# All large tiles moved to multiples of 2 KB, and the head norms computed with the tokens in the partitions

## What is computed

```python
def rms_norm(x, g):
    y = xf * lax.rsqrt(jnp.mean(xf * xf, axis=-1, keepdims=True) + EPS)
    return (y * g).astype(x.dtype)

# first layer: h = rms_norm(x, norm_mix); h @ w_in is split into heads
aq = rms_norm(aq.reshape(b, t, 4, 2, 64), a_q_norm)      # ak alike; heads of 64
out_a = rms_norm(diff_attention(aq, ak, av, ...), a_subln)   # 4 heads of 128
bq = rms_norm(bq.reshape(b, t, 3, 4, 128), b_q_norm)     # bk alike; windowed attention
ck = rms_norm(kv[:, :, 0], c_k_norm)                     # 256 memory tokens
cq = rms_norm(cq.reshape(b, t, 4, 128), c_q_norm)
x = x + sum(gates * branches) @ w_out
x = x + (silu(h2 @ w_ffn_gate) * (h2 @ w_ffn_up)) @ w_ffn_down
# second and third layer, each:
x = x + 0.5 * swiglu(rmsnorm(x, ...), w1, w3, w2)
o = hgrn2_chunkwise(q, k, v, log_f)                      # 4 heads of 128
o = o * lax.rsqrt(jnp.mean(o * o, axis=-1, keepdims=True) + EPS) * norm_g * silu(g_in)
x = x + concat(o, multiscale_pool(u)) @ w_out
x = x + mem_cross_attention(rmsnorm(x, ...), rmsnorm(mem, ...), wq, wkv, wo)
x = x + 0.5 * swiglu(rmsnorm(x, ...), w1, w3, w2)
return rmsnorm(x, final_norm)
```

## Time and profile before

| | before |
|---|---|
| median of 3 runs | 3494.8 us (3493.5 to 3494.88) |
| the profiled execution | 3494.81 us, span 3493.0 us |
| TensorE busy, matmuls | 3339.0 us (96%) |
| TensorE busy, weight loads | 2691.4 us (77%) |
| VectorE busy | 1876.8 us (54%) |
| ScalarE busy | 1110.6 us (32%) |
| mean granted clock of TensorE | 0.982 |
| memory traffic | 313.41 MB, mean 90 GB/s |

### The profile page before, as it was taken

How to read it: one execution, slowest core, us unless ns; L and a number is a source line. 1 busy time by engine, 2 the same in 40 slices (tenths; PEclk the granted TensorE clock), 3 DMA queues, 4 the chain that set the end, 5 groups by cost and what they waited for, 6 DMA issues and landing times. The chain is left out here.

```text
span 3493.0 us, 39914 instructions
## 1 busy us (share of the span) xinstructions
PE 3339.0 (96%) x15102; PEld 2691.4 (77%) x15102; DVE 1876.8 (54%) x2458; ACT 1110.6 (32%) x1487; POOL 0.2 (0%) x4
## 2 busy tenths in 40 slices
PE   7889999999999999999899999999999989999998
PEld 6657777768888888888786888888888868778886
DVE  6666666555554455335764555345543576555543
ACT  3543444433222322232333322222222233332221
POOL 0000000000000000000000000000000000000000
PEclk9989999999999999999899999999999989999999
DMA  3222222322222222222231222222222223222222
GB/s 130 88 68 85 89 83 73 103 87 94 96 96 97 94 97 97 91 100 74 74 101 55 91 96 96 96 91 96 96 96 98 80 67 103 67 79 96 96 94 81
DMA packets 88824, 313.41 MB, mean 90 GB/s; under 512 B 9984, under 2 KB 10496, under 8 KB 88448
## 3 DMA queue, kind: packets, MB, share of 16 engines
q1 hardware_dynamic: 82080, 294.69, 25.3%
q10 hardware_dynamic: 6624, 17.03, 1.6%
HBM read 309.58 MB, written 2.10 MB: 89 GB/s over the span
## 5 line engine op out<-in xcount | busy, mean ns | idle before, releaser
L784 PE MATMUL ps<-x_hi,whi 128*128 128x512 f32 x2816 | 1121.8, 398 | 13.1 <-DVE wlo L1193 13.1
L786 PE MATMUL ps<-x_hi,wlo 128*128 128x512 f32 x2816 | 1101.0, 391 | 0.0
L785 PE MATMUL ps<-x_lo,whi 128*128 128x512 f32 x2816 | 1100.8, 391 | 0.0
L1011 ACT ACTIVATE whi<-raw 128x1024 fp32r<-128x1024 f32 x554 | 582.7, 1054 | 988.3 <-DMA raw<-in_weights 985.6
L1193 DVE TENSOR_TENSOR wlo<-raw,whi 128x1024 fp32r<-128x1024 f32 x554 | 676.1, 1222 | 374.5 <-ACT whi L1011 366.3
L784 PEld LDWEIGHTS ps<-x_hi,whi 128*128 128x128 f32 x2816 | 532.6, 189 | 132.7 <-DVE wlo L1193 13.2
L785 PEld LDWEIGHTS ps<-x_lo,whi 128*128 128x128 f32 x2816 | 532.5, 189 | 113.3 <-issue 5.7
L786 PEld LDWEIGHTS ps<-x_hi,wlo 128*128 128x128 f32 x2816 | 531.5, 189 | 113.3
L786 PE MATMUL ps<-h_hi,wlo 128*128 128x512 f32 x880 | 346.7, 394 | 0.0
L784 PE MATMUL ps<-h_hi,whi 128*128 128x512 f32 x880 | 346.7, 394 | 0.0
L785 PE MATMUL ps<-h_lo,whi 128*128 128x512 f32 x880 | 346.7, 394 | 0.0
(11 more groups left out here) (249 smaller groups left out, 3065.1 us busy)
## 6 DMA issues: line engine op xcount, KB each, us to landing
raw<-in_weights SPq DMA_DIRECT2D x554, 512.0 KB, 3.3
bias<-in_biasB ACTq DMA_DIRECT2D x16, 384.0 KB, 3.3
bias<-in_biasA ACTq DMA_DIRECT2D x16, 256.0 KB, 3.6
x_res<-in_x SPq DMA_DIRECT2D x8, 256.0 KB, 6.2
x_res<-in_x ACTq DMA_DIRECT2D x1, 2048.0 KB, 9.3
out_x<-x_res SPq DMA_DIRECT2D x8, 256.0 KB, 2.1
mem_raw<-in_mem ACTq DMA_DIRECT2D x1, 1024.0 KB, 4.6
mem_raw2a<-in_mem ACTq DMA_DIRECT2D x2, 512.0 KB, 3.9
```

The lines of the kernel that those rows point to most:

```text
L784: pe.matmul(out, hi, xhi, start=start, stop=False)
L785: pe.matmul(out, hi, xlo, start=False, stop=False)
L786: return pe.matmul(out, lo, xhi, start=False, stop=stop)
L1011: return act.activation(out, in_, ACT.Copy, scale=scale)
```

## The change

**Addresses.** The constants and small tiles are laid first, then the address is rounded up to a multiple of 2 KB, and the ring, x, x_hi, x_lo, `rstd_x`, `sq_sum` and `sq` follow. In the program as built `raw` is at 20480, x_hi at 69632, x_lo at 86016, `sq` at 106496 and the arena at 110592, all multiples of 2048; the arena's tiles keep their offsets in it. `rstd_mem` moves into the arena. The `rec` and `h_rec` tiles are gone.

**Head norms.** The square is now the stationary operand and a column of ones the moving one, for each block of 128 tokens: four small products (`hsum`) give the 128 x 4 sums with the tokens in the partitions (128 x 8 for A, two halves each). They go into a few columns of a PSUM bank of the jobs, the one after the next to be written. VectorE turns them into mean plus EPS and takes their reciprocal (`hinv`, 4 or 8 columns), ScalarE takes the root while it spreads each column over 128 (or 64) elements into `sd`, TensorE transposes the four blocks of `sd` into `O` (`hturn`), and VectorE multiplies the head by gain and `O` (`hscale`). Where there were two deferred steps in one flush there are now two flushes: sums one job after the square, transposes and scaling another job later. `settle` puts the inverses at the start of the next job; `drain` flushes until nothing is deferred.

**Order.** In `b_jobs` the value column of group 1 goes behind the keys of group 2, the last value column of the first head goes before the last split of A, and in the second pair of the mixer two key jobs of the memory move ahead of the scalings.

```diff
@@ class Schedule
+    def settle(self):
+        inverses, self.inverses = self.inverses, []
+        for id, form in inverses:
+            self.step("hinv", id=id, form=form, last=inverses[-1][0])
+        self.groups += 1
+
+    def hsums(self, id, ones, n, dim, sq):
+        form = dict(nt=n // P, w=2 if ones == "halves" else 1, dim=dim, slot=self.nsums % 4, k=self.nsums, group=self.groups)
+        self.nsums += 1
+        self.step("hsum", id=id, ones=ones, sq=sq, form=form, bank=(self.njobs + 1) % 3, behind=self.njobs - 2)
+        self.inverses.append((id, form))
+        return form
+
+    def hscale(self, id, form, /, **a):
+        self.settle()
+        self.step("hturn", id=id, form=form)
+        self.step("hscale", id=id, **a)
...
-        def rest():
-            step("hnorm", id=id, ones=ones, n=n, dim=dim, sq=sq)
-            step("hscale", id=id, src=src, gain=gain, n=n)
-        s.defer(rest)
+        def sums():
+            form = s.hsums(id, ones, n, dim, sq)
+            s.defer(lambda: s.hscale(id, form, src=src, gain=gain, n=n))
+        s.defer(sums)
...
-        return out
+        return [out[k] for k in (0, 1, 2, 3, 4, 6, 7, 5, 8)]
...
-    s.flush()
+    s.drain()
...
+        top[0] = (top[0] + 2 * KB - 1) // (2 * KB) * (2 * KB)
         raw_at = top[0]
...
@@ tensor
-                elif kind == "hnorm":
-                    pe.wait_ge(*on("hsq", a["id"]))
-                    wait_free("O")
-                    pe.matmul(O[:, 0:a["n"]], lhs[:, :], SQ[:, a["sq"], 0:a["n"]], start=True, stop=True)\
-                        .then_inc(*sig("hsum", a["id"]))
-                    free["O"] = ("hsd", a["id"])
+                elif kind == "hsum":
+                    pe.wait_ge(*on("hsq", a["id"]))
+                    if a["behind"] >= 0:
+                        pe.wait_ge(*on("evac", a["behind"]))
+                    picks = halves[:, 0:P:P // 2] if a["ones"] == "halves" else ones[:, 0:1]
+                    for c in range(form["nt"]):
+                        mm = pe.matmul(out[:, c * w:(c + 1) * w], SQ[:, a["sq"], c * P:(c + 1) * P], picks,
+                                       start=True, stop=True)
+                elif kind == "hturn":
+                    pe.wait_ge(*on("hsd", a["id"]))
+                    wait_free("O")
+                    for c in range(a["form"]["nt"]):
+                        mm = pe.transpose(O[:, c * P:(c + 1) * P], sd[:, c * P:(c + 1) * P], ident[:, :])
+                    free["O"] = ("hn", a["id"])
@@ scalar
-                    act.activation(sd[:, 0:a["n"]], O[:, 0:a["n"]], ACT.Sqrt, bias=EPS, scale=1.0 / a["dim"])
+                    act.activation(sd.rearrange("p (a b) -> p a b", a=cells),
+                                   inverse_of(form).rearrange("p (a b) -> p a b", b=1)
+                                   .broadcast_to([P, cells, P // form["w"]]), ACT.Sqrt).then_inc(*sig("hsd", a["id"]))
@@ vector
-                    dve.reciprocal(rec[:, 0:n], sd[:, 0:n]).then_inc(*sig("hrec", a["id"]))
+                    dve.wait_ge(*on("hsum", a["last"]))
+                    dve.tensor_scalar(inv, sums_at(sum_bank[a["id"]], form), 1.0 / form["dim"], EPS, ALU.mult, ALU.add)
+                    dve.reciprocal(inv, inv).then_inc(*sig("hinv", a["id"]))
...
-                    dve.scalar_tensor_tensor(buf(a["src"]), buf(a["src"]), gain_of(a["gain"]), rec[:, 0:n],
+                    dve.wait_ge(*on("hrt", a["id"]))
+                    dve.scalar_tensor_tensor(buf(a["src"]), buf(a["src"]), gain_of(a["gain"]), O[:, 0:n],
                                              ALU.mult, ALU.mult).then_inc(*sig("hn", a["id"]))
```

95 lines of the change are left out of this document (64 added, 31 removed).

## The result

The changed kernel takes 3455.47 us (median of 4 runs, 3454.62 to 3458.89), the kernel before, beside it, 3494.15 us (4 runs). The ratio is 0.989, with a 95% interval from 0.9877 to 0.9902: 39 us faster, where 164 were forecast. The profiled execution has a span of 3453.4 us. Lines have moved: the three products of a weight tile are now at 827, 828 and 829 (784, 785 and 786 before), the sums of the head norms at 889, their transposes at 898, ScalarE's root at 1148, VectorE's small pair at 1371 and 1374, the final multiply at 1379.

A forecast was written before the change was run, and what follows sets the result against it. TensorE, busy 96% of the span, was taken as the bound. From 3494.8 us, 162 for aligned addresses (172 less 10 given back) and 2 for head norms gave 3331 us, range 3297 to 3505.

The forecast's parts named there:

- The aligned product, 215 ns: Weight products with 512 columns: starts 215 ns apart once tiles are 2 KB-aligned, from 226.7 (x) and 233.3 (arena).
- its 95 us: Products reading x_hi or x_lo: 8110 at full clock, each 11.7 ns shorter, saving 95 us.
- the arena's 69 us: Products reading arena tiles (h, mix, xo, y, branch outputs): 3888 x 0.97, each 18.3 ns shorter, saving 69 us.
- Rival 1: 13 ns stay with every fp32r product, only the arena's 6.7 ns vanish: 26 us, 3467 us; chance 0.20 (3365 to 3475).
- The choice between two forms at offset 0: Aligned fp32r products: either no address loss, taken as 215 ns, or a loss of 64 columns, 240 ns.
- Products with 256 columns, 8 us: The shorter weight products: 768 save 9 ns each, 7 us, and the other 192 about 1 us.
- 10 us given back: Attentions and mixers, where TensorE waits for other engines: faster products only wait longer, cutting the address gain to 162 us.
- The head norms, -2 us: All 52 head norms: 22 us of transposes plus 4 of new waits less 28 of shorter waits; ends -20 and +25.
- the 9 us in each mixer: Recurrent mixers: some 9 of 21.9 us TensorE idle time in each vanish without the long reciprocal.
- the 10 us in the attentions: The two attentions: a quarter of TensorE's 41.3 us idle time saved, taken as 10 us.
- The new waits: Transposes waiting for sum, inverse and root where no job lies between: 3 us some four times, less earlier waits, 4 us.
- rival 2: Addresses do nothing: 3493 us, with the norms' ends 3475 to 3518; chance 0.10 together with rival 4, costlier norms.

The follow-up runs named there:

- The probe: Straight-line programs on TensorE alone, groups of 24 products with tile and weight addresses varied; fp32r with 512 columns took 226.7 ns at equal places, mostly 232.5 to 234.5 otherwise.
- the addresses alone: The kernel before with only the new 2 KB-aligned addresses and its old head norms: 3474.35 us, ratio 0.9942.
- the first program: Straight-line TensorE program in place of the model, 36 groups of 24 products varying offsets, columns, weight widths and types; fp32r with 512 columns took 226.7 ns at offset 0.
- the copies: New addresses with old head norms, each of the 52 VectorE reciprocals replaced by a plain copy of the same 512 elements: 3409.55 us, ratio 0.9756.
- a version 30 us faster: New addresses, old-form head norms without transposes, ScalarE making the inverse root by ln and exp from one table: 3425.07 us, ratio 0.9798.

## Why the prediction failed, by its steps

**The aligned product, 215 ns: wrong, and this is the miss.** It measures 226.7. The step took the 13.3 ns at x's offset for a part of the same address cost as h's 20 ns, and let both vanish at 0. The probe shows two costs: a fixed 13 ns of every fp32r product at the upper clock, and 6.7 ns where the moving tile and the weights stand differently in their 256 bytes. x paid only the first, so its 95 us were nothing; of the arena's 69 us there were 26 by the products and 20.4 by the clock on the wall. Rival 1 had this sum, 26 us and 3467, and its 0.20 was too low: it rested on "no row here is below 226.7 for fp32r", the only evidence of the right type, while the forecast leaned on a plain fp32 row. That row was true (214.6 ns a pass) and said nothing of fp32r.

**The choice between two forms at offset 0** had "64 less the elements past the boundary" against no loss. Neither: the address of one tile is not what counts. The front part had the clue, since the weights stood at 128 bytes just as x did. The prediction named the weights' place only at its end, as a danger ("if aligned tiles meet the aligned weights in the same place"); the same place is the fast one.

**Products with 256 columns, 8 us: nothing.** They are fastest with unequal places (117.8 ns), and 120.0 now.

**10 us given back** in the waiting stages: right in kind, 5.5 of the 8.3 us of those stages' arena products.

**The head norms, -2 us: -19 measured against the addresses alone, inside the ends of -20 and +25.** That it is inside is luck. The transposes were put at 22 us; that is what they take, and they cost some 17. The sums, 0.89 us, were right: in the first program plain fp32 records with 2 columns are 111.7 ns apart (L715), eight of them 0.89 us. The gain was put at 28 us and is 64.8 by the copies. Of the waits, the 9 us in each mixer were right (9.2 and 10.8 us less idle time); the 10 us in the attentions, a quarter of their idle time by guess, were too few, since some 24 of the 43.5 us lie in the first layer. The other 22 us are the clock: that fewer waits could bring it up the sum had at nothing. The new waits were put at 4 us, after "some four times"; they are 25.6 us in 12 places and cost 14 to 16, with some 11 more in the chain. In the terms of the account above, 17 + 14 + 11 - 61 = -19 us stands where 22 + 4 - 28 = -2 stood: terms that were off by 5, 21 and 33 us, the larger two against each other.

**The clock and the order.** That the drains might stall TensorE was named as a way to be wrong; they do (waits of up to 4.8 us), without a lower clock: the mean granted clock went from 0.982 to 0.987.

**A slip that moved nothing.** The ends of rival 2 are 3475 and 3520 us by its own sum (3494.8 + 25), not 3518.

**The range**, 3297 to 3505, held the time only since it took in rival 1; the own range of the forecast, 3300 to 3365, did not.

## What to carry over

Before an address is blamed, write down where each operand of the slow and of the fast instruction stands: here the pair decided, and 64 bytes did what aligning every tile did. A price from another data type is no bound for this one; a small straight-line program with one variable per group of 24 products settles in one run what no reading of the kernel's trace can. And to find what a long instruction is worth, put a short one of the same reads, writes and waits in its place: 64.8 us came out where adding up the waits had given 28, a third of it by the clock, and it led to a version 30 us faster than a cure which costs TensorE some 17 us by its transposes and 14 to 16 by waits. Before a saving is booked as the price of what was taken away, look whether it lies in the stages where that stood: 3.5 of the 16.2 us did not.

## What the runs showed of the hardware

- An fp32r product with 512 columns takes 226.7 ns at 2.4 GHz at best, with 384 columns 173.3, with 256 119.7: 13 ns above its columns. With 480 columns it takes 216.9, 16.9 above. bf16 takes 215.8 and plain fp32 214.6 a pass, at both places of the moving tile that were tried (0 and 832 bytes, weights at 0).
- Weights and moving tile at the same place modulo 256 bytes: 226.7 to 227.8 ns; the moving tile 64 bytes further: 228.7 to 228.9; otherwise 231.9 to 234.5. The place in the 256 bytes does not count by itself: 226.7 to 226.9 with both at 0, 32, 64, 96, 128 or 192.
- With 256 columns the order is reversed: 120.0 ns with both at 128, 117.8 with the weights at 128 and the moving tile at 832.
- A reciprocal of 512 elements per partition on VectorE takes 3353 ns and a copy of the same 427.
- Every load of an activation table takes ScalarE 1283 ns, and one table can hold ln and exp: 98 loads fewer in the program were worth 19 us.
- A stretch at the lower clock in the memory attention cost 1.7 us: in 21 us from nearly the same point TensorE does 59 records at a mean granted clock of 0.92 and 66 at 1.00.
